# A joint stage of attention and delta rule: another order of units, shorter steps, and level masks made by GpSimd

## The reference, cut to what matters

```python
def _masked_softmax(s, mask): ...                   # max, exp, sum
no = gate[:, :, 0] * o_cmp + gate[:, :, 1] * o_sel + gate[:, :, 2] * o_win
no = no.reshape(B, T, NSA_WIDTH) * jax.nn.silu(pr['nsa_g'])
# delta rule, one chunk:
A = eye + jnp.where(strict, jnp.einsum('bihd,bjhd->bhij', kb, kc) * L, 0.0)
Tinv = lax.linalg.triangular_solve(A, eye, left_side=True, lower=True)
u = Tinv @ (vc * bc);  w = Tinv @ (kb * exp(G))
v_new = u - w @ S
o = (qc * exp(G)) @ S + ((qc @ kc.T) * L) @ v_new
S = S * exp(G_last) + (kc * exp(G_last - G)).T @ v_new
```

## Time and profile before

| | us |
|---|---|
| median of 3 runs | 2557.96 |
| lowest and highest run | 2548.28, 2562.9 |
| profiled execution | 2549.31 |
| its span, first to last instruction | 2547.4 |
| first joint stage | 362.0 to 731.2 |
| second joint stage | 1626.0 to 1994.2 |
| TensorE busy over the span | 2200.4 (86%) |
| VectorE, ScalarE, GpSimd busy | 1268.9, 797.8, 342.8 |

### The profile page before, as it was taken

How to read it: one execution, slowest core, us unless ns; L and a number is a source line. 1 busy time by engine, 2 the same in 40 slices (tenths; PEclk the granted TensorE clock), 3 DMA queues, 4 the chain that set the end, 5 groups by cost and what they waited for, 6 DMA issues and landing times. The chain is left out here.

```text
span 2547.4 us, 35903 instructions
## 1 busy us (share of the span) xinstructions
PE 2200.4 (86%) x12280; PEld 1629.6 (64%) x12280; DVE 1268.9 (50%) x2972; ACT 797.8 (31%) x1646; POOL 342.8 (13%) x586
## 2 busy tenths in 40 slices
PE   6999768888779999997889997578787799999977
PEld 3644446677757888885355544457676588888853
DVE  2253464555535666664213543545655456666532
ACT  2221112233334554440212111123434344445302
POOL 0110000000032432420001100000000333344100
PEclk9999768798868999996989997578988799999869
DMA  5452100000065886863045411000000768678431
GB/s 187 165 182 66 37 23 1 9 1 1 2 147 144 187 183 152 185 131 111 2 151 176 164 58 37 23 1 9 1 1 24 163 146 185 158 175 189 93 111 37
DMA packets 173052, 243.06 MB, mean 95 GB/s; under 512 B 50714, under 2 KB 132282, under 8 KB 172192
## 3 DMA queue, kind: packets, MB, share of 16 engines
q1 hardware_dynamic: 143328, 147.27, 22.4%
q0 software_dynamic: 29536, 93.43, 14.1%
HBM read 223.69 MB, written 25.50 MB: 98 GB/s over the span
## 5 line engine op out<-in xcount | busy, mean ns | idle before, releaser
L609 PE MATMUL bank<-W,hT 128*128 128x512 f32 (+3 forms) x1152 | 447.8, 540 | 12.6 <-DMA W<-in_w_in 9.1
L1035 POOL DMA_DIRECT2D SHARED<-in_cache_nsa_kv x256 | 152.8, 597 | 1488.4 <-issue 1079.2
L609 PEld LDWEIGHTS bank<-W,hT 128*128 128x128 f32 x1152 | 216.9, 195 | 201.4 <-issue 172.0
L978 PE MATMUL bank<-XT,W 128*128 128x256 f32 (+1 forms) x768 | 250.8, 462 | 0.0
L967 ACT ACTIVATE XT<-bank 128x512 f32<-128x512 f32 x256 | 140.3, 593 | 137.6 <-PE bank L960 137.6
L1035 POOL DMA_DIRECT2D PS<-in_cache_nsa_kv x256 | 150.9, 589 | 139.4 <-issue 126.7
L978 PEld LDWEIGHTS bank<-XT,W 128*128 128x128 f32 x768 | 135.2, 190 | 49.5 <-issue 36.8
L1411 DVE TENSOR_REDUCE mx<-bank 128x1 f32<-128x31 f32 (+4 forms) x192 | 74.9, 390 | 182.3 <-PE bank L1263 180.8
L960 PE MATMUL bank<-CF,RP 128*128 128x128 f32 x1024 | 148.2, 292 | 9.8 <-DVE RP L948 8.7
L1223 ACT ACTIVATE Pr<-bank,mx 128x31 f32<-128x31 f32 (+4 forms) x192 | 85.7, 447 | 203.1 <-DVE mx L1412 202.7
L1692 PEld LDWEIGHTS bank<-PB,PS 128*128 128x128 f32 x1024 | 132.7, 210 | 10.6 <-issue 6.7
(11 more groups left out here) (396 smaller groups left out, 3656.4 us busy)
## 6 DMA issues: line engine op xcount, KB each, us to landing
SHARED<-in_cache_nsa_kv SPq DMA_DIRECT2D x256, 128.0 KB, 5.8
SHARED<-in_cache_nsa_kv POOLq DMA_DIRECT2D x256, 128.0 KB, 5.4
PS<-in_cache_nsa_kv SPq DMA_DIRECT2D x256, 128.0 KB, 6.1
PS<-in_cache_nsa_kv POOLq DMA_DIRECT2D x256, 128.0 KB, 5.7
W<-in_w_in SPq DMA_DIRECT2D x48, 512.0 KB, 3.7
XS<-scratch_conv_p POOLq DMA_DIRECT2D x24, 384.0 KB, 4.5
PW<-in_state_nsa_win SPq DMA_DIRECT2D x16, 512.0 KB, 3.8
Wo<-in_w_out SPq DMA_DIRECT2D x4, 2048.0 KB, 11.9
```

The costliest lines, as they stand in the source:

```text
L609: return nc.tensor.matmul(bk((c * NTILE + t) % BANKS)[:, 0:b - a], hT[:, k, t * P:(t + 1) * P], W[:, k // 2, k % 2, 0:b - a], start=(k == ...
L978: mm = nc_(self.v).tensor.matmul(out, self.v['W1'][:, kv, s, :], seg[:, s], start=(s == 0), stop=(s == SEG // PAIRS - 1))
L1035: e.dma_start(where[side * HD:(side + 1) * HD, slot, :, :], A['cache_nsa_kv'][l, page].rearrange("(p r) a g d -> p r (a g d)", r=PAIRS)[:, ...
```

## The change

The order of the delta tiles is now 0, 4, 1, 2, 3, and only tile 0 is made ready ahead of the levels. Steps are shorter: `prep` is cut off from `ready0`, the normalization is `norm0` and `norm1`, tile 4's masks are `mask0` and `mask1`, and its state additions four steps. TensorE waits for VectorE's step before only at steps with products that need it (`PRODUCTS`). Units go by rows, then heads, then branches; the tiles of rows come as 3, 0, 1, 2; two units stand at the very start. The products of two heads in three branches (a group of 6 units) stand in the PSUM bank; ScalarE copies them to SBUF, and VectorE scales, sums and gates them there. GpSimd makes all 31 masked matrices NTs, in two buffers, each as soon as NTt is there and the matrix two levels earlier is used up.

In the diff, the pieces after the planner are GpSimd's, ScalarE's, TensorE's (two) and VectorE's, in this order.

```diff
-    TILES = (4, 0, 1, 2, 3)
+    TILES = (0, 4, 1, 2, 3)
...
-    state = lambda t: [(f"state{i}", t) for i in range(5 if t == 4 else 4)]
-    beside = {4: [], 0: state(4) + ready(1), 1: state(0) + ready(2), 2: state(1) + ready(3), 3: state(2)}
-    DELTA = ready(4) + ready(0)
+    ready = lambda t: [(n, t) for n in ("prep", "ready0", "ready1", "ready2")]
+    state = lambda t: [(n, t) for n in ("state0", "state1", "state2", "norm0", "norm1")]
+    sampled = [("mask0", 4), ("mask1", 4)] + state(4) + [(n, 4) for n in ("add00", "add01", "sums1", "add10", "add11")]
+    beside = {0: ready(4), 4: state(0) + ready(1), 1: sampled + ready(2), 2: state(1) + ready(3), 3: state(2)}
+    DELTA = ready(0)
...
-    QTS, BRANCHES, DEEP, AHEAD = (3, 2, 1, 0), (1, 2, 0), 2, 0.93
-    units = [(qt, br, h) for qt in QTS for br in BRANCHES for h in range(NH)]
+    QTS, BRANCHES, DEEP, AHEAD = (3, 0, 1, 2), (1, 2, 0), 2, 0.95
+    units = [(qt, br, h) for qt in QTS for h in range(NH) for br in BRANCHES]
+    NU, GROUP = len(units), 6
...
-    cost = [P + keys(u) for u in range(NU)]
-    ORDER, spent, u = [], 0, 0
+    cost = [2 * P + keys(u) for u in range(NU)]
+    ORDER, spent, u = [("unit", 0), ("unit", 1)], cost[0] + cost[1], 2
...
+            for i, (t, k) in enumerate(steps):
+                n = ROWS[t]
+                dve.wait(e, f"nt1{t}")
+                if i >= 2:
+                    t2, k2 = steps[i - 2]
+                    dve.wait(e, f"tt{t2}.{k2}")
+                pool.done(e, f"nn{t}.{k}", nc.gpsimd.tensor_tensor(NTs(t, k)[0:n, :, 0:n], NTt_[t][0:n, :, 0:n],
+                                                                   b_(cf('level', P)[0:n, k, 0:n], 1, [n, H4, n]), ALU.mult))
             dve.wait(e, "n33")
             first_pages(e, A, l, v, 1)
...
+                if u >= 2 and (u - 2) % GROUP == GROUP - 1:
+                    k = (u - 2) // GROUP
+                    e.wait_ge(used, u - 1)
+                    if k:
+                        e.wait_ge(freed, k)
+                    nc.scalar.activation(OB[:, :, :, :].rearrange("p h b d -> p (h b d)"), bk(OUT)[:, 0:GROUP * HD], ACT.Copy).then_inc(merged, 1)
...
+                    pool.wait(e, f"nn{t}.{s}")
+                    at = steps.index((t, s))
+                    if at:
+                        dve.wait(e, "tt%d.%d" % steps[at - 1])
...
-                dve.wait(e, before)
+                if what in PRODUCTS or (what, t) == ("norm0", 4):
+                    dve.wait(e, before)
...
+                    e.wait_ge(merged, k + 1)
+                    link(nc.vector.tensor_scalar(fac[:, :, :], SUM[:, k % 2, :, :], 1e-30, None, ALU.max))
+                    link(nc.vector.reciprocal(fac[:, :, :], fac[:, :, :]))
+                    link(nc.vector.tensor_tensor(fac[:, :, :], fac[:, :, :], gates, ALU.mult))
+                    link(nc.vector.tensor_tensor(OB[:, :, :, :], OB[:, :, :, :], b_(fac[:, :, :], 3, [P, 2, 3, HD]), ALU.mult))
+                    nc.vector.tensor_reduce(NO[:, :, :], OB[:, :, :, :].rearrange("p h b d -> p h d b"), AX.X, ALU.add).then_inc(freed, 1)
```

More of the change, by code:

```diff
@@ L1097, in delta_attention @@
     kd_ = sb(scope, "kd", [P, SETS, 256])
-    work = sb(scope, "work", [P, 5, H4, P])
-    NTs, M1, T, gb, LT = (work[:, i, :, :] for i in range(5))
+    work = sb(scope, "work", [P, 6, H4, P])
+    NTs_, (M1, T, gb, LT) = [work[:, i, :, :] for i in range(2)], (work[:, 2 + i, :, :] for i in range(4))
+    steps = [(t, k) for t in TILES for k in range(LEVELS[t])]
+    NTs = lambda t, k: NTs_[steps.index((t, k)) % 2]
     QM = [U[2][:, i * 512:(i + 1) * 512] for i in range(3)] + [U[3][:, 0:512]]
@@ L1137, in delta_attention @@
             if what == "turn":
-                dn += [f"ns{t}.0"] if s == 0 else [] if last else [f"nn{t}.{s}"]
                 pn += [f"a{t}.{s}"]
@@ L1146, in delta_attention @@
         if what == "ready0":
[L1147 removed]
+            dn += [f"{n}{t}" for n in ("g0", "g1", "g3", "gd", "lt")]
             pn += [f"{n}{t}" for n in ("g", "gr")]
             an += [f"{n}{t}" for n in ("eg", "el", "sl", "L0", "L1", "L2", "L3")]
+        if what == "prep":
+            dn += [f"{n}{t}" for n in ("kb", "vb", "gb")]
         if what == "ready1":
@@ L1156, in delta_attention @@
         if what == "state0":
-            dn += ([f"qm{i}" for i in range(4)] if t == 4 else []) + [f"{n}{t}" for n in ("ks", "r")]
+            dn += [f"{n}{t}" for n in ("ks", "r")]
             pn += [f"ks{t}"]
@@ L1165, in delta_attention @@
             pn += [f"av{t}", f"su{t}"] if t < 4 else [f"av{t}"]
-        if what == "state3":
-            dn += [f"{n}{t}" for n in ("sq", "va", "rc", "n1", "n2", "n3")]
+        if what == "norm0":
+            dn += [f"{n}{t}" for n in ("sq", "va")]
             an += [f"rt{t}"]
-        if t == 4 and what in ("state3", "state4"):
-            q = int(what == "state4")
-            pn += [f"sv{q}"]
-            dn += [f"ss{hp}{q}{j}" for hp in range(2) for j in "nms"] + ([] if q else ["vm1"])
+        if what == "norm1":
+            dn += [f"{n}{t}" for n in ("rc", "n1", "n2", "n3")]
+        if what in ("mask0", "mask1"):
+            dn += [f"qm{2 * int(what[-1]) + i}" for i in range(2)]
+        if t == 4 and what in ("norm0", "sums1"):
+            pn += [f"sv{int(what == 'sums1')}"]
+        if what[:3] == "add":
+            q, hp = int(what[3]), int(what[4])
+            dn += [f"ss{hp}{q}{j}" for j in "nms"] + (["vm1"] if what == "add01" else [])
         ends[what, t] = dn[-1]
-    with stage(["dve_s", "act_s", "pe_s", "loaded", "gl", "outs", "kv", "score", "shift", "exped", "turned", "copied", "used", "link_s", "merged"]) as \
-            (block, (dve_s, act_s, pe_s, loaded, gl, outs, kv, score, shift, exped, turned, copied, used, link_s, merged)):
+    with stage(["dve_s", "act_s", "pe_s", "loaded", "gl", "outs", "kv", "score", "shift", "exped", "turned", "copied", "used", "link_s", "merged", "freed", "masked"]) as \
+            (block, (dve_s, act_s, pe_s, loaded, gl, outs, kv, score, shift, exped, turned, copied, used, link_s, merged, freed, masked)):
         dve, act, pe = Steps(dve_s, dn), Steps(act_s, an), Steps(pe_s, pn)
+        pool = Steps(masked, [f"nn{t}.{k}" for t, k in steps])
         @block.sync
@@ L1468, in _ @@
                 hb = lambda ap: b_(ap, 2, [n, H4, HD])
-                if what == "ready0":
+                if what == "prep":
                     dve.done(e, f"kb{t}", nc.vector.tensor_tensor(h3(kb[0:n, :]), h3(y[:, 256:512]), hb(u[:, GB:GB + H4]), ALU.mult))
@@ L1472, in _ @@
                     dve.done(e, f"gb{t}", nc.vector.tensor_copy(gb[0:n, :, :], b_(g_log[0:n, t, :], 2, [n, H4, P])))
+                if what == "ready0":
                     pe.wait(e, f"g{t}")
@@ L1495, in _ @@
                 if what == "state0":
-                    for i in range(4) if t == 4 else ():
-                        dve.link(e, f"qm{i}", nc.vector.tensor_tensor(QM[i], b_(QKT[:, i, 0:64], 1, [P, NB, 64]), cf('own', 64), ALU.mult))
                     pe.wait(e, f"ks{t}")
@@ L1500, in _ @@
                     dve.link(e, f"r{t}", nc.vector.tensor_tensor(T1[0:n, 256:512], vb[0:n, :], T1[0:n, 0:256], ALU.subtract))
+                if what in ("mask0", "mask1"):
+                    for i in range(2 * int(what[-1]), 2 * int(what[-1]) + 2):
+                        dve.link(e, f"qm{i}", nc.vector.tensor_tensor(QM[i], b_(QKT[:, i, 0:64], 1, [P, NB, 64]), cf('own', 64), ALU.mult))
                 if what == "state1":
```

102 lines of the change are left out of this document (39 added, 63 removed).

## The result

The changed kernel took 2512.8 us, the kernel before 2553.1 us beside it: a ratio of 0.986, 95% interval 0.983 to 0.990. It is faster, by 40 us where 80 were forecast, and lies outside the forecast's own range of 2430 to 2500 us. The change is 1.4%, and executions of one kernel lie 5 to 37 us apart in what follows.

A forecast was written before the change was run, and what follows sets the result against it. In the joint stage TensorE, the busiest engine, idles 76 us per layer at mean clock 0.80, with slow short-unit runs. Terms -53-5+6+4+2+3+3 = -40 per layer, -80 from 2549.3, plus 3: 2472 us; range 2430 to 2500.

The forecast's parts named there:

- the first term: Joint stage: new unit order, shorter steps and ready-made masks save 53 us per layer, middle of 39.5 and 66.
- The clock half: First term's upper end: joint-stage work runs at the 512 to 578 us rate, saving 66 us per layer; clock above 0.85.
- The waits half: First term's lower end: 39.5 us per layer of TensorE's waits in the joint stage lose their cause, clock unchanged.
- only the waits go: Rival, joint stages: clock stays, only the waits' lower end counts, -26.5 us per layer, 2499 us; chance 0.22.
- the 330 us of the forecast: Sign that the forecast is right: the joint stages take about 330 us each.
- Start, -5: Stage start: two units, about 7 us, replace 11.8 us of readying tile 4 first; 5 us less per layer.
- Tail, +6: Stage end: the new tail takes 17 us against about 11 at the good rate; 6 us more per layer.
- Merging, +4 and +2: Merging per layer: half of VectorE's 8 us more on the path, +4; ScalarE's value-bank copies, +2.
- Masks, +3 and +3: GpSimd's masks, 1.2 us each: TensorE's wait for each tile's first, +3; VectorE slowed beside them, +3, per layer.
- The upper end, 55 us: Upper bound on masks' cost to VectorE: each of 31 masks stops VectorE for its whole length.
- The moved stretch: Rival: short units now beside tile 1 make a slow stretch there; +12 us per layer, 2576 us; chance 0.09.
- the calm case: Within the moved-stretch rival: TensorE's work beside tile 1 takes 154 us in place of 85.

The follow-up runs named there:

- e4: Changed kernel without the first two units ahead of tile 0's preparation; units are dealt between its steps. 0.980 of before, 10.1 us per stage won.
- e8: e4 with units dealt out evenly up to the last small step, so fewer stand alone in the tail; 0.977 of before.
- e10: e8 with each merging's six units ordered branch 1, 2, 0, both heads of each, instead of head by head; 0.9751 of before, stages 331 us.
- e14: Changed kernel with merging of the units' results left out but for a column; 19.7 us per stage won.
- e17: Changed kernel with most of the merging moved from VectorE to GpSimd; stage 15.6 us shorter.
- e5a: e4 with unused identity products on TensorE ahead of the tail's waits for exponentials and copied transposes; tail 3.7 us shorter, whole-time intervals overlap.
- e2: Changed kernel with VectorE making the masked matrices again, one step ahead; stage 5.0 us longer than the changed kernel's, 11.4 us shorter than before.
- e6: Changed kernel with GpSimd making each masked matrix twice; 5.7 us per stage lost.
- e9: e4 with sampled-state additions cut into two steps and each merging dealt to two units; 15.6 us lost against e4.
- e9a: e8 with only each merging of six units dealt to two of them; stages 345.9 and 337.7 us, 6.4 us longer than e8's.

## Why the prediction was right in its direction and wrong in its size

**The step that failed** is the first term, "I take the middle, 53 us", between 39.5 us of waits and 66 us of work at the rate of the good stretch. With the other terms as forecast, together +13, the 16.4 us that came leave 29 of the 53, less than its lower end. The clock half hardly came: 0.83 and 0.81 for 0.80, below the 0.85 named, and TensorE's busy time did not fall. The waits half came, and more than half of it was given back: nearly all of the 39.5 us of named waits are gone, but TensorE's idle time fell by 17 us only, since the waits for exponentials (+12.1), for copied transposes (9.7, before 5.1), for GpSimd (+3.4) and others stand in their place. The nearest case is the rival "only the waits go", 2499 us, and even that kept too much. Its own ground, "a step that waited for one engine often waits for the next", is what happened.

**Why the clock did not come.** The forecast read low clocks as runs of short units. Those runs are gone, and the lowest clocks that are left stand at the stage's ends, here the first 40 us and the last 35 (beside tile 1 it is 0.91):

```profile
368.50:388.50 20.00, 11.53 (x44) 7.49 (x44) 8.55 (x21) 5.06 (x13) 0.82 (x1) 0.50 0.17 41
388.50:408.50 20.00, 17.69 (x92) 15.02 (x93) 7.67 (x22) 6.06 (x20) 3.18 (x3) 0.67 0.00 1
...
685.00:700.00 15.00, 12.93 (x59) 10.59 (x60) 7.11 (x22) 6.75 (x15) 0.00 (x0) 0.60 0.03 6
700.00:720.30 20.30, 15.12 (x56) 11.12 (x54) 6.78 (x23) 5.75 (x17) 4.75 (x8) 0.50 0.42 104
```

That the clock could be had is shown by e4, e8 and e10 (0.85, 0.87 and 0.89), which change only the order of units; e10 reaches the 330 us of the forecast by it. Why the clock is higher in these orders was not found. VectorE is busy 54% of the stage, and I read that as room; by e14 and e17 a us of its work cost 0.6 to 0.8 us in the changed order, and in e10's order nothing. In the changed kernel its busy time fell by 5.3 us only (196.8 to 191.5): the masks took 20.5 us off it, the merging put 9 on (23.0 to 32.4), and rows beside masks grew by about 7.

**Start, -5.** I counted two units of 3 us in front against 11.8 us for tile 4. Up to both first norms the stage is 5.6 us shorter (155.8 for 161.4), with the masks in it; by e4 the two units in front put the preparation 5.5 us later and cost 9.7. The change lost more there than the term gave, and 10 of the 24 us per layer that are missing from the forecast came back in e4.

**Tail, +6.** 17 us were worked out, 20.2 came, against 28.0 before with more units in it. The long units were counted at a duration from a stretch at 0.95, and TensorE stands at 0.50 there; e5a gives 3.7 us of it back.

**Merging, +4 and +2.** Half of 8 us on the path; VectorE's work grew by 9.4, and at the 0.6 to 0.8 of e14 and e17 that is 6 to 8 us, an estimate. The term was mis-sized by little; the whole merging costs 20 us per stage by e14, which I did not look at.

**Masks, +3 and +3.** The duration (1.29 against 1.2) and TensorE's wait for first masks (3.4 us) were right. VectorE's rows grew beside them as estimated: against e2, where GpSimd makes no mask, the same instructions took 6.9 and 7.2 us more in the two layers, where 6 were worked out. All of it lies in ten instructions of a stage that began during a mask and ended only behind it. One, with its mask, and then a group that has three of the ten, in the changed kernel and in e2:

```profile
591.98 1.27 POOL L1219 TENSOR_TENSOR work<-UP,SHARED 128x512 f32<-128x512 f32 x1 [6.87 <-DVE UP L1475]
...
592.17 1.36 DVE L1538 TENSOR_TENSOR T<-Ot 128x256 f32<-128x256 f32 x1
```
```profile
L1507 DVE TENSOR_TENSOR gs<-gs,UP 128x4 f32<-128x4 f32 x4 | 2.5, 624 | 0.0
```
```profile
L1502 DVE TENSOR_TENSOR gs<-gs,UP 128x4 f32<-128x4 f32 x4 | 0.6, 150 | 0.0
```

The square of line 1538 takes 0.42 us without a mask. Eight of the ten read two SBUF operands; rows that read a PSUM bank took their usual time during a mask (line 1506: 0.41 us). The trace agrees with the rule of the Trainium skill (SBUF — State Buffer, "Who interferes with whom"), by which a VectorE instruction with two SBUF inputs and a GpSimd instruction that reads SBUF block each other. The upper end, 55 us, is far off because so few instructions meet a mask in this way. What share of the 7 us is on the path was not measured. The doubled masks of e6 lengthened VectorE's work by another 2.6 us.

**The moved stretch** did not decide: beside tile 1 the clock was 0.91, with 77 us, where 85 were reckoned at the good rate and 154 for the calm case. e9 shows that it can, with other steps.

## What to carry to other kernels

A busy share of half on an engine is not room, when its queue is in order and stands inside a short chain of other engines: price what is put on it or taken off it by the chain, and test that by moving the same work to an idle engine. The price holds for that order alone: here the same move gave 15.6 us in one order and nothing in another. Waits named in a profile are not gains to be added up; ask of each which wait is next, and count at most the idle time that no other chain needs. Count TensorE's idle time and its busy time apart, since a gain can lie in either. Look at the first and last 20 us of a stage by themselves, and at what the next stage waits for, before shortening them.

## What the runs showed of the hardware that was not expected

In the tail TensorE stayed at 1.2 GHz though its busy share was 15.0 of 20.2 us; with unused products between (13.8 of 16.5) it stayed at 2.4 (0.99). GpSimd's operations on two inputs took 1293 ns over 512 columns, 861 over 384 and 462 to 535 over 128, where VectorE took 690, 558 and 292. A VectorE product over 4 columns took 0.78 us where it began during a mask, and 0.15 in e2. One instruction stream took 345.9 and 337.7 us in the two layers of one execution (e9a), with a mean clock of 0.81 and 0.85.
